# Experts taken in an order by token count, and a shorter router, in a decoder layer on one core

## The chip, the cores and the metric

The kernel runs on one core of a Trainium2 chip. A core has TensorE for matrix products, VectorE, ScalarE and GpSimd (POOL) for element-wise work, and SyncE (SP), which here issues nearly all DMA transfers. The metric is the time of one execution in device microseconds; lower is better.

## The reference, cut to what matters

One layer over 256 tokens of width 1024 in float32: a mixer (gated delta rule and differential attention), a cross-attention over 256 memory tokens, and a mixture of experts, each followed by `x = LN(alpha*x + h)`. The change concerns the end of the second part and the third:

```python
x = layer_norm(DEEPNORM_ALPHA * x + mem_cross_attention(x, mem, ...), ln2_g, ln2_b)
logits = xt @ router_w + router_b                 # 32 experts
top_val, top_idx = lax.top_k(logits, 4)           # 4 experts for each token
gate = softmax(top_val)
h = clamped_swiglu(xb @ w_gate[e] + b_gate[e], xb @ w_up[e] + b_up[e])
y = h @ w_down[e] + b_down[e]                     # for the tokens that chose expert e
x = layer_norm(DEEPNORM_ALPHA * x + sum of gate * y, ln3_g, ln3_b)
```

Each expert has three matrices of 4 MB, 12.6 MB (six halves of 2 MB) in all. With the reference's inputs the 32 experts get 24, 13, 39, 39, 69, 64, 35, 47, 60, 16, 16, 28, 27, 25, 53, 44, 27, 18, 6, 31, 39, 36, 25, 36, 14, 49, 28, 14, 25, 33, 28 and 16 tokens.

## The kernel before, in words

The five engines run five written-out programs, joined by semaphores. Up to the router everything is a fixed list of "units" (`unit_table`): each unit fills one of the eight banks of PSUM from TensorE and is emptied by ScalarE or VectorE; the list's order is TensorE's order and says which bank is free when.

**Cross-attention's end and the router.** The output product W_o has four units of eight products each (`wo0` to `wo3`: two blocks of 128 tokens by two halves of 512 columns). VectorE adds each to the residual (`residual`, L1643) and gathers statistics; `standardise` (L1632) takes the variance, waits for POOL's root (L568) and scales the block. TensorE transposes the scaled block (`x2T0` to `x2T3`), ScalarE and VectorE copy it with gain and bias applied, and eight products for each block give the logits (`route_block`, L1207). Small products on the identity (`keep_warm`, L1217) fill waits. VectorE picks the four largest of 32 (L1705 to L1717). Gains and biases of the block itself are applied by VectorE (block 0, `gains`, L1650) and POOL (block 1, L579 to L581), and TensorE puts alpha times x into four accumulator banks (L1236), where all expert outputs are added later.

**Tables.** A product with a triangle of ones gives each token's position in its expert's list (`pos`, L1241 to L1245). Expert lists are cut into blocks of 32 slots. VectorE counts blocks for each expert (`nblk`, L1741), TensorE sums them up to each expert (`cum`, L1273) and makes a table that says, for each block, whose it is (`etab`, L1287). VectorE writes both tables as integers to `itab` and raises `tab_ready` (L1779). These three small steps are called inside block 0, behind its first, second and fourth eighth of gate and up products (`tables`, L1289), with the transposes of the gates (`GT`) as the second.

**The loop over blocks.** For each block (`work`, L1302) TensorE makes gate and up products (64 of 512 columns, L1318), gathers the next block's tokens (L1255), transposes, adds the previous block's output to the accumulators (L1297), and makes the down products in two passes of 16 (L1359). VectorE and ScalarE do bias, clamp, sigmoid and copies between.

**The loader.** Experts are taken by number, 0 to 31. Weights of even experts go to one set of six slots, of odd experts to another, so two experts are on chip at a time. SP (`load_expert`, L498) reads from `itab` how many blocks come up to and with the expert two before, waits until that many blocks have used the slot, and issues: first halves of gate and up (G0, U0) behind `gu0_used`, second halves (G1, U1) behind `gu_done`, the down halves D0 and D1 behind `d0_used` and `y_done`. The halves of experts 0 and 1 are loaded ahead, at fixed places in cross-attention (L477 to L491), into memory that has come free there. Before the first load of expert 2, SP waits for `tab_ready` (L492).

Of the kernel before, what the change touches and what calls it, by code (L numbers as in the profile page):

```python
# [21 lines left out]
I32 = mybir.dt.int32  # L22
ALU = mybir.AluOpType
# [31 lines left out]
TABLE = 64  # L55
MAX_BLOCKS = N_EXPERTS + SEQ * TOP_K // CAP
# [7 lines left out]
K_ID, K_IOTA, K_UT, K_US, K_ONE, K_CM, K_SOLVE = 0, 128, 192, 320, 448, 576, 960  # L64
N_CONST = K_SOLVE
S_EYE, S_BLOCK, S_LEVT = 0, 256, 260
N_SOLVE = S_LEVT + P * (LEVELS - FIRST_LEVEL)
K_END = K_SOLVE + N_SOLVE


def constants():
# [11 lines left out]
    out[:, K_IOTA:K_IOTA + TABLE] = np.arange(TABLE)  # L83

# [19 lines left out]
def unit_table():  # L104
# [21 lines left out]
    u += [("xs3", "D"), ("vm2", "A"), ("pT0", "A"), ("pT1", "A"), ("vm3", "A"), ("pT2", "A"), ("oT0", "A"), ("oT1", "A")]  # L126
    u += [("pT3", "A"), ("oT2", "A"), ("oT3", "A")]
    u += [("wo0", "D"), ("wo1", "D"), ("wo2", "D"), ("x2T0", "A"), ("x2T1", "A"), ("wo3", "D"), ("bT", "A")]
    u += [("x2T2", "A"), ("x2T3", "D"), ("router", "D")] + [(f"acc{i}", "kept") for i in range(4)]
    u += [("pos", "D"), ("xg0", "A"), ("xgT0", "D"), ("cum", "D"), ("GT", "A"), ("etab", "D")]  # L130
# [6 lines left out]
LAST_USE = {"xgT0": "pos", "cum": "router", "GT": "x2T3", "etab": "GT"}  # L137
# [14 lines left out]
def emptied(name):  # L152
# [12 lines left out]
    ("xa_wo", 0, 1024, 0), ("xa_wo", 0, 1024, 1),  # L165
# [6 lines left out]
ROLE_SLOT = [(N_ATT + r) % SLOTS for r in range(SLOTS)]  # L172
# [6 lines left out]
def trunk_kernel(nc, d, out):  # L179
    ctx = ExitStack()  # L180
    with ctx:
# [32 lines left out]
        small = sb("small", 696)  # L214
        itab = sb("itab", TABLE + 32, I32)

# [41 lines left out]
        iota = kst[:, K_IOTA:K_IOTA + TABLE]  # L258
        levT = {level: ln_mem[:, S_LEVT + P * i:S_LEVT + P * (i + 1)] for i, level in enumerate(range(FIRST_LEVEL, LEVELS))}
# [39 lines left out]
        shift_fin = take(1)  # L299
        top8 = take(16)  # L300
        gsum = take(2)
        nblk, cumc = take(2), take(2)
        rb = take(32)
        eps_rms = take(1)
        minus_half = take(4)
        logit, expl, M, G, pos = (take(64) for _ in range(5))
        assert at[0] <= 696
# [14 lines left out]
        dnw_keep = sb("dnw_keep", 128)  # L322

# [8 lines left out]
        erow = conv_in[0:1, 576:640]  # L332
        mg, mu = (conv_in[:, 256 * i:256 * (i + 1)].rearrange("p (j f s) -> p j f s", j=4, f=2) for i in (4, 5))
        router_w = conv_in[:, 2048:2048 + KC * N_EXPERTS]
        xgT = conv_in[:, 2304:2560].rearrange("p (v h u s) -> p v h u s", v=2, h=2, u=2)
# [10 lines left out]
        T_E, T_CUM = 0, TABLE  # L346
# [30 lines left out]
        ld_cols = sem("ld_cols")  # L377
        gu0_used = sem("gu0_used")
# [24 lines left out]
        rt_in, rt_exp = sem("rt_in"), sem("rt_exp")  # L403
        route_ready = sem("route_ready")
# [27 lines left out]
        def _(sp):  # L432
# [6 lines left out]
            def load_needed_later():  # L439
# [5 lines left out]
                sp.dma_start(ln_mem[:, 0:N_SOLVE], d["consts"][:, K_SOLVE:K_END]).then_inc(ld_lev, 16)  # L445
# [17 lines left out]
            def load_role(role, e, odd, ahead=0):  # L463

                w = d[ROLE_INPUT[role]][0, ahead:].rearrange("e (h p j) n -> e h p (j n)", h=2, j=4)
# [6 lines left out]
            def load_first(role):  # L472
                sp.wait_ge(ring_used, N_ATT + role - SLOTS + 1)
                load_role(role, 0, odd=False)
# [15 lines left out]
            sp.wait_ge(ln_ready, 4)  # L490
# [3 lines left out]
            def blocks_through(e, ahead=0):  # L494

                return sp.value_load(itab[0:1, bass.ds(e + (T_CUM + ahead), 1)], min_val=1, max_val=MAX_BLOCKS)

# [96 lines left out]
        def _(act):  # L594
# [209 lines left out]
            for i in range(3):  # L804
                if i == 2:
                    empty("bT", ebias, as3(2))
# [1083 lines left out]
```

## Time and profile before

| | us |
|---|---|
| median of 3 runs (lowest, highest) | 1252.56 (1250.12, 1252.93) |
| profiled execution, its own time | 1252.49 |
| its span, first to last instruction | 1250.4 |
| TensorE busy | 1089.8 (87%) |
| VectorE busy | 317.5 (25%) |
| ScalarE busy | 189.5 (15%) |
| POOL busy | 35.7 (3%) |
| DMA | 446.56 MB, 357 GB/s over the span |

The page cuts the span into 40 slices of 31.3 us, with the busy share of each engine as a digit (9 is 90% or more). Windows give the same for any stretch, with the granted clock of TensorE as a share of full speed and the DMA's rate. The chain of waits follows the work that ended last back through what released it. A busy share is a mean over stages with different limits.

### The profile page before, as it was taken

Reading aid. Unit: us, or ns where it says so; the run is one execution under the profiler, and the core shown is the slowest. Engines: PE = TensorE matmul, PEld = TensorE weight load, DVE = VectorE, ACT = ScalarE, POOL = GpSimd, SP = SyncE. Lnnn points to the kernel's source line nnn. Section 1 sums busy time; section 2 is a strip of 40 time slices with the busy share of each in tenths; the row PEclk is TensorE's granted clock in tenths of the full one; section 3 lists DMA queues with packets and bytes.
Section 4 is the critical chain, followed back from the end, with each engine's and each line's share of the span. In section 5 each row is a group of like instructions: output and inputs, shape, how many; then the busy total and the mean of one; then the engine's idle time right before and its main releaser. Section 6 shows DMA issues by size and latency. Waiting matters only on the chain.

```text
span 1250.4 us, 19511 instructions
## 1 busy us (share of the span) xinstructions
PE 1089.8 (87%) x7535; PEld 493.7 (39%) x7536; DVE 317.5 (25%) x973; ACT 189.5 (15%) x433; POOL 35.7 (3%) x38
## 2 busy tenths in 40 slices
PE   8999999999899999999966789776699797967885
PEld 6777874965433333333312223222233232322321
DVE  1757433213322222222211122111122221211123
ACT  1231331121111111111100011100011111100111
POOL 0110010100100000000000000000000000000001
PEclk9999999999999999999988799878799898987988
DMA  9733140557899989999999999999999999999995
GB/s 363 275 138 135 68 157 20 202 221 301 347 429 429 429 345 403 408 401 409 428 428 429 429 428 429 430 429 428 428 428 428 428 429 428 429 430 429 428 428 234
DMA packets 43687, 446.56 MB, mean 357 GB/s; under 512 B 6912, under 2 KB 7376, under 8 KB 19088
## 3 DMA queue, kind: packets, MB, share of 16 engines
q1 hardware_dynamic: 39616, 442.43, 84.5%
q10 hardware_dynamic: 4048, 3.81, 1.0%
q8 instruction: 15, 0.25, 0.1%
q14 instruction: 8, 0.07, 0.0%
HBM read 445.18 MB, written 1.05 MB: 357 GB/s over the span
## 4 chain that ended last, share of the span: by engine, by line
PE 60%; DMA 25%; DVE 5%; issue 3%; another core or an unknown queue 2%; DVEq 2%; SPq 1%; POOL 0%; POOLq 0%; ACT 0%; ACTq 0%
DMA main<-in_exp_w_up_dram 24%; PE bank L1318 23%; PE bank L1359 10%; PE bank L882 8%; PE bank L872 6%; PE bank L1255 2%; PE bank L1346 2%; PE bank L1122 2%; DVEq L1807 1%; DVE kst L1813 1%; DVE main L1810 1%; DVE main L1800 1%; PE bank L931 1%; DMA main<-in_w_in_dram 1%
## 5 line engine op out<-in xcount | busy, mean ns | idle before, releaser
L1318 PE MATMUL bank<-main 128*32 128x512 f32 x3008 | 392.0, 676 | 122.2 <-DMA main<-in_exp_w_up_dram 117.7
L1318 PEld LDWEIGHTS bank<-main 128*32 128x32 f32 x3008 | 113.3, 122 | 393.8 <-issue 360.1
L1359 PE MATMUL bank<-main,kst 128*32 128x512 f32 x1504 | 180.8, 598 | 16.9 <-DVE kst L1813 16.9
L1800 DVE TENSOR_TENSOR main<-bank,main 128x256 f32<-128x256 f32 x94 | 39.6, 421 | 590.9 <-PE bank L1346 590.9
L882 PE MATMUL bank<-main 128*128 128x512 f32 x256 | 111.8, 593 | 0.3 <-ACT main L693 0.3
L815 ACT ACTIVATE main<-bank 128x512 f32<-128x512 f32 x47 | 28.1, 598 | 479.2 <-PE bank L1318 479.2
L1297 PE MATMUL bank<-main 64*128 64x512 f32 x384 | 95.4, 615 | 0.7 <-ACT main L823 0.7
L872 PE MATMUL bank<-main 128*128 128x256 f32 x352 | 77.8, 380 | 0.0
L1359 PEld LDWEIGHTS bank<-main,kst 128*32 128x32 f32 x1504 | 39.3, 109 | 90.1 <-issue 64.1
L882 PEld LDWEIGHTS bank<-main 128*128 128x128 f32 x256 | 48.2, 190 | 56.7 <-issue 56.5
L872 PEld LDWEIGHTS bank<-main 128*128 128x128 f32 x352 | 66.5, 190 | 10.1 <-issue 1.1
L1255 PE MATMUL bank<-main,kst 128*32 128x256 f32 x768 | 53.2, 389 | 1.2 <-DVE kst L1733 1.0
L617 ACT ACTIVATE main<-bank 128x512 f32<-128x512 f32 (+2 forms) x51 | 28.2, 578 | 146.5 <-PE bank L872 66.0
L1791 DVE TENSOR_SCALAR main<-kst,small 128x128 f32<-128x128 f32 x94 | 22.7, 284 | 101.4 <-PE bank L1367 99.7
L1297 PEld LDWEIGHTS bank<-main 64*128 64x128 f32 x384 | 33.1, 186 | 29.8 <-issue 22.5
L821 ACT ACTIVATE main<-bank 128x256 f32<-128x256 f32 x47 | 18.0, 383 | 170.7 <-PE bank L1367 170.7
L1255 PEld LDWEIGHTS bank<-main,kst 128*32 128x32 f32 x768 | 27.0, 109 | 38.0 <-issue 28.5
L568 POOL TENSOR_TENSOR small<-small 128x1 f32<-128x1 f32 (+1 forms) x10 | 7.8, 782 | 1088.4 <-DVE small L1833 921.9
L823 ACT ACTIVATE main<-bank 128x512 f32<-128x512 f32 x47 | 28.1, 597 | 70.5 <-PE bank L1359 70.5
L1346 PE MATMUL bank<-kst,main 128*128 128x128 f32 x188 | 35.1, 310 | 0.0
L1346 PEld LDWEIGHTS bank<-kst,main 128*128 128x128 f32 x188 | 26.2, 209 | 20.4 <-issue 20.4
L1261 PEld LDWEIGHTS bank<-kst,main 128*128 128x128 f32 x96 | 15.1, 207 | 36.6 <-issue 35.6
(252 smaller groups left out, 707.0 us busy)
## 6 DMA issues: line engine op xcount, KB each, us to landing
main<-in_exp_w_gate_dram SPq DMA_DIRECT2D x64, 2048.0 KB, 30.2
main<-in_exp_w_up_dram SPq DMA_DIRECT2D x64, 2048.0 KB, 34.7
main<-in_exp_w_down_dram SPq DMA_DIRECT2D x64, 2048.0 KB, 36.7
main<-in_w_in_dram SPq DMA_DIRECT2D x6, 2048.0 KB, 21.8
main<-in_xa_wk_dram SPq DMA_DIRECT2D x2, 2048.0 KB, 10.4
main<-in_w_out_dram SPq DMA_DIRECT2D x2, 2048.0 KB, 10.9
main<-in_xa_wv_dram SPq DMA_DIRECT2D x2, 2048.0 KB, 10.9
main<-in_xa_wq_dram SPq DMA_DIRECT2D x2, 2048.0 KB, 13.7
```

Of the source, the lines that this page charges most:

```text
L617: act.activation(dst, ps[:, :] if src is None else src(ps), func, **kw).then_inc(act_emptied, 1)
L815: act.activation(gu_sb, gu_bank[:, :], ACT.Copy).then_inc(gu_copied, 1)
L823: act.activation(y_sb, y_bank[:, :], ACT.Copy).then_inc(y_copied, 1)
L872: last = pe.matmul(ps[:, j * SEQ:(j + 1) * SEQ], w(k)[:, c * P:(c + 1) * P], src[:, k, :], start=(k == 0), stop=(k == KC - 1))
L882: last = pe.matmul(ps[:, :], srcT[:, k, b * P:(b + 1) * P], w(k)[:, col:col + 512], start=(k == 0), stop=(k == KC - 1))
L1122: last = pe.matmul(ps[:, j * SEQ + b * P:j * SEQ + (b + 1) * P], w(k)[:, (2 * i + j) * P:(2 * i + j + 1) * P], xT[:, k, b * P:(b + 1) * P] ...
L1255: last = pe.matmul(ps[at:at + CAP, 0:256], selw[:, b, :], quarters[:, h, u, :, :], start=(b == 0), stop=(b == 1))
L1297: last = pe.matmul(acc[b][h][:, :], gselT[64 * h:64 * h + 64, b * P:(b + 1) * P], y_sb[64 * h:64 * h + 64, :], start=False, stop=final)
L1318: last = pe.matmul(gu_bank[at:at + CAP, :], xg_chunk(k), weights(role, k, f), start=(k == 0), stop=(k == KC - 1))
L1346: last = pe.transpose(guT_bank[:, j * P:(j + 1) * P], gu_sb.rearrange("p (c j) -> p j c", j=4)[:, j, :], ident)
L1359: last = pe.matmul(y_bank[at:at + CAP, :], hT[:, j, f, :], weights(role, j, h), start=(f == 0 and pair == 0), stop=(f == 1 and pair == 1))
L1800: return tt(dst, gT[:, :, w, :, :], b.unsqueeze(3).broadcast_to([P, 4, 2, CAP]), ALU.add)
```

## The change

- Experts are no longer taken by number. VectorE ranks them by token count (experts 0 and 1 are kept first, ties go to the lower number), a constant row says which rank stands at which position (few and many in turn, the one with fewest last), and the tables get a second row: for each block its position (`T_P`) and its expert (`T_E`), and for SP the expert at each position (`T_ORDER`). Slots go by parity of the position. SP reads one table entry more for each expert.
- The router works on the residual before the norm: its weights are multiplied by LN's gain, their column mean is subtracted (`rw`, a product with ones), the bias part goes into the router's bias, and the logits are scaled by the block's 1/std afterwards. So the transposes don't wait for the norm.
- W_o goes in the order 0, 2, 1, 3 with the transposes between, from two loads cut by columns instead of rows. `keep_warm` is gone, `bT` (biases of the experts) moves ahead to cross-attention.
- Block 0's gains and biases go in two fused instructions on VectorE; block 1 is standardised by ScalarE, and its gains and biases are applied by POOL (lower half) and VectorE (upper half).
- Accumulator sums 1, 2 and 3 move behind `pos` and the gather. The gathered rows are copied by ScalarE. The gates' transposes move behind block 0's gate and up products.
- Early loads: G0 and U0 of expert 0 come behind `xq3`, D0 of expert 1 with its G1 and U1; which memory follows which load is a new list (`ROLE_FOLLOWS`).

```diff
+def rank_at_position():
+    heavy, light = list(range(FIRST_EXPERTS, 16)), list(range(16, N_EXPERTS))
+    last = light.pop()
+    order = list(range(FIRST_EXPERTS))
+    while heavy or light:
+        if light:
+            order.append(light.pop())
+        if heavy:
+            order.append(heavy.pop(0))
+    return np.array(order + [last])
...
+    tie = np.where(e < FIRST_EXPERTS, 1e6 * (FIRST_EXPERTS - e), 0.0) - e
...
-    ("xa_wo", 0, 1024, 0), ("xa_wo", 0, 1024, 1),
+    ("xa_wo", 0, 512, None), ("xa_wo", 512, 512, None),
...
+ROLE_FOLLOWS = [13, 14, 11, 12, 15, 16]
+ROLE_RELEASES = [13, 13, 15, 15, 16, 17]
...
             load_role(G0, 1, odd=True)
+            load_first(G0)
+            load_first(U0)
             sp.wait_ge(unit_filled, UNIT_AT["xs3"] + 1)
             load_role(U0, 1, odd=True)
-            for role in (G0, U0, G1, U1):
-                load_first(role)
+            load_first(G1)
+            load_first(U1)
             sp.wait_ge(unit_filled, UNIT_AT["oT3"] + 1)
             load_role(G1, 1, odd=True)
             load_role(U1, 1, odd=True)
+            load_role(D0, 1, odd=True)
             load_first(D0)
             load_first(D1)
-            sp.wait_ge(unit_filled, UNIT_AT["router"] + 1)
-            load_role(D0, 1, odd=True)
-            sp.wait_ge(ln_ready, 4)
+            sp.wait_ge(ln_ready, 5)
             load_role(D1, 1, odd=True)
             sp.wait_ge(tab_ready, 1)
...
+                done = blocks_through(p, ahead - 2)
+                e = sp.value_load(itab[0:1, bass.ds(p + (T_ORDER + ahead), 1)], min_val=0, max_val=N_EXPERTS - 1)
...
+            root(6, rstd_fin[0])
+            root(7, rstd_fin[1])
+            pool.wait_ge(ld_ln, 64)
+            pool.wait_ge(scaled_x, 1)
+            pool.tensor_tensor(x3[:, 1, 0:HALF], x3[:, 1, 0:HALF], ln_g[:, 0:HALF], ALU.mult)
+            pool.drain()
+            pool.tensor_tensor(x3[:, 1, 0:HALF], x3[:, 1, 0:HALF], ln_b[:, 0:HALF], ALU.add).then_inc(ln_ready, 1)
...
+            arrived(15)
+            ps = begin("wo0")
+            need("oT2")
+            wo_steps(ps, 0, range(0, 6))
+            need("oT3")
+            wo_steps(ps, 0, range(6, 8)).then_inc(unit_filled, 1)
+            wo_steps(begin("wo2"), 2, range(0, 8)).then_inc(unit_filled, 1)
+            need("wo0")
+            tokens_T("x2T", 0, x3)
+            used_up(1, "wo2")
+            arrived(16)
+            wo_steps(begin("wo1"), 1, range(0, 8)).then_inc(unit_filled, 1)
+            need("wo2")
+            tokens_T("x2T", 2, x3)
+            bank_wo3 = begin("wo3")
+            wo_steps(bank_wo3, 3, range(0, 4))
+            need("wo1")
+            tokens_T("x2T", 1, x3)
+            wo_steps(bank_wo3, 3, range(4, 8)).then_inc(unit_filled, 1)
...
+            pe.wait_ge(ln_ready, 5)
             gather(begin("xg0")).then_inc(unit_filled, 1)
+            begin_sum(2)
+            begin_sum(3)
             need("xg0")
             gathered_T(begin("xgT0")).then_inc(unit_filled, 1)
...
                 for k in range(4):
                     last = gate_up(k)
+                    if first and k == 1:
+                        block_counts()
+                last.then_inc(gu0_used, 1)
+                if first:
+                    block_table()
...
+            def choose(b):
+                top = top8[:, 8 * b:8 * b + 8]
+                stt(l3[:, b, :], filled(f"rt{b}")[:, 0:N_EXPERTS], rstd_fin[b], rb, ALU.mult, ALU.add).then_inc(dve_emptied, 1)
+                if b == 1:
+                    stt(offset, mv_fin[1][:, 0:1], -1.0, rstd_fin[1], ALU.mult, ALU.mult).then_inc(offset_in, 1)
...
+            upper_half = slice(HALF, D_MODEL)
+            dve.wait_ge(scaled_x, 2)
+            tt(x3[:, 1, upper_half], x3[:, 1, upper_half], ln_g[:, upper_half], ALU.mult)
+            dve.drain()
+            tt(x3[:, 1, upper_half], x3[:, 1, upper_half], ln_b[:, upper_half], ALU.add).then_inc(ln_ready, 1)
...
+            stt(keys, counts_ps[0:32, 96:128], 64.0, key_row, ALU.mult, ALU.add)
+            stt(own_key, counts_ps[0:32, 64:65], 64.0, key_col, ALU.mult, ALU.add)
+            ts(filling, counts_ps[0:32, 64:65], 1.0 / CAP, None, ALU.mult)
+            dve.drain()
+            dve.sem_inc(dve_emptied, 1)
+            ts(keys, keys, own_key, None, ALU.is_gt)
+            ts(block_steps, iota[0:32, 1:SEQ // CAP], filling, None, ALU.is_lt)
+            dve.drain()
+            dve.reduce_sum(rank, keys, AX_X)
+            dve.reduce_sum(nblk[0:32, 0:1], block_steps, AX_X)
+            dve.drain()
+            stt(at_rank, rank_at[:, 0:32], rank, iota[0:32, 0:32], ALU.is_equal, ALU.mult)
+            ts(at_position, rank_at, rank, None, ALU.is_equal)
```

## Rows read from the trace of the kernel before

**Rows 1.** Page: tenths busy in 40 slices of the span.
```profile
PE   8999999999899999999966789776699797967885
DMA  9733140557899989999999999999999999999995
```
**Rows 2.** Windows: stretch, length; busy PE, PEld, DVE, ACT, POOL; clock, DMA share, GB/s.
```profile
335.00:340.00 5.00, 4.83 (x48) 1.90 (x42) 1.63 (x7) 1.69 (x3) 0.00 (x0) 1.00 0.69 226
340.00:450.00 110.00, 106.47 (x902) 37.94 (x900) 26.79 (x93) 17.51 (x37) 0.00 (x0) 1.00 1.01 428
450.00:620.00 170.00, 165.24 (x1406) 58.76 (x1404) 40.22 (x141) 25.85 (x55) 0.00 (x0) 1.00 0.95 396
620.00:1230.00 610.00, 481.24 (x3586) 160.48 (x3584) 104.47 (x364) 66.58 (x140) 0.00 (x0) 0.89 1.01 429
```
**Rows 3.** Chain of waits: start us, us, what.
```profile
618.70 46.42 DMA main<-in_exp_w_up_dram
1047.08 6.11 PE bank L1318 x32
1223.27 5.06 PE bank L1318 x32
```
**Rows 4.** Chain of waits: down products and gate and up products of full blocks.
```profile
391.56 1.85 PE bank L1359 x16
393.70 7.07 PE bank L1318 x64
422.86 1.85 PE bank L1359 x16
```
**Rows 5.** Timeline of SP: start us, us, line, transfer; first gate halves.
```profile
335.72 0.35 SPq L470 DMA_DIRECT2D main<-in_exp_w_gate_dram  x1
350.90 0.33 SPq L470 DMA_DIRECT2D main<-in_exp_w_gate_dram  x1
413.02 0.33 SPq L470 DMA_DIRECT2D main<-in_exp_w_gate_dram  x1
459.44 0.34 SPq L470 DMA_DIRECT2D main<-in_exp_w_gate_dram  x1
```
**Rows 6.** Timeline from W_o to the tables.
```profile
279.65 20.76 PE L882 MATMUL bank<-main 128*128 128x512 f32 x48
300.25 1.04 PE L864 MATMUL bank<-kst,main 128*128 128x128 f32 x8
308.20 0.69 DVE L1646 SCALAR_TENSOR_TENSOR main<-main,bank 128x512 f32<-128x512 f32 x1 [2.89 <-PE bank L882]
318.19 0.23 DVE L1705 TENSOR_TENSOR small<-bank,small 128x64 f32<-128x64 f32 x1 [1.68 <-PE bank L1211]
320.17 1.96 PE L1236 MATMUL bank<-main,kst 128*128 128x512 f32 x4 [0.22 <-POOL main L581]
321.97 0.30 PE L1241 MATMUL bank<-small,kst 128*128 128x32 f32 x2
323.37 0.51 DVE L1733 TENSOR_SCALAR kst<-kst,small 128x32 f32<-128x32 f32 x2
325.54 0.32 PEld L1261 LDWEIGHTS bank<-kst,main 128*128 128x128 f32 x2 [1.01 <-ACT main L617]
327.27 0.42 DVE L1763 COPY main<-bank 128x256 f32<-128x256 f32 x1
327.80 1.32 PE L1318 MATMUL bank<-main 128*32 128x512 f32 x8 [1.75 <-DVEq L1766]
334.32 0.18 DVE L1777 CAST itab<-main 1x64 int32<-1x64 f32 x1
```
**Rows 7.** Timeline of the end: POOL and VectorE at the same time.
```profile
1243.44 1.25 POOL L590 TENSOR_TENSOR main<-main 128x512 f32<-128x512 f32 x1
1243.64 1.61 DVE L1838 TENSOR_TENSOR main<-main 128x512 f32<-128x512 f32 x1
```
**Rows 8.** DMA issues: transfer, queue, KB, median us to landing.
```profile
main<-in_router_w_dram ACTq DMA_DIRECT2D x1, 128.0 KB, 8.0
```

More of the change, by code:

```diff
@@ L299, in trunk_kernel @@
         shift_fin = take(1)
+        offset = take(1)
         top8 = take(16)
@@ L302, in trunk_kernel @@
         nblk, cumc = take(2), take(2)
+        filling, own_key, rank, position = (take(1)[0:N_EXPERTS, :] for _ in range(4))
         rb = take(32)
@@ L1202, in _ @@
-            last.then_inc(unit_filled, 1)
-            pe.wait_ge(ld_rt, 32)
-            router_ps = begin("router")
-            def route_block(b, parts=()):
-                for k in range(KC):
-                    if k in dict(parts):
-                        need(dict(parts)[k])
-                    last = pe.matmul(router_ps[:, 32 * b:32 * b + 32], xT[:, k, b * P:(b + 1) * P], router_w[:, 32 * k:32 * k + 32],
+            pe.wait_ge(rsum_ready, 1)
+            pe.matmul(begin("rw")[:, 0:2 * N_EXPERTS], ones, router_sums, start=True, stop=True).then_inc(unit_filled, 1)
@@ L1212, in route_block, with wo_steps @@
+            wo_w = [slots[i % SLOTS].rearrange("p k n -> p (k n)").rearrange("p (k n) -> p k n", k=KC) for i in (15, 16)]
+            def wo_steps(ps, i, steps):
+                for k in steps:
+                    last = pe.matmul(ps[:, :], oT[:, k, (i // 2) * P:(i // 2 + 1) * P], wo_w[i % 2][:, k, :],
                                      start=(k == 0), stop=(k == KC - 1))
                 return last
-            warm_bank = begin("acc0")
-            def keep_warm(products):
-                for _ in range(products):
-                    pe.matmul(warm_bank[:, 0:P], ident, ident, start=True, stop=True)
@@ new lines, in _, with route @@
+            need("wo2")
+            tokens_T("x2T", 2, x3)
+            bank_wo3 = begin("wo3")
[3 more added lines that the diff above has]
+            wo_steps(bank_wo3, 3, range(4, 8)).then_inc(unit_filled, 1)
+            def route(ps, b, steps):
+                for k in steps:
+                    last = pe.matmul(ps[:, 0:N_EXPERTS], x2T[b][:, k, :], router_w3[:, k, :], start=(k == 0), stop=(k == KC - 1))
+                return last
@@ new lines, in begin_sum @@
+            def begin_sum(i):
+                pe.matmul(begin(f"acc{i}")[:, :], alpha_eye, x3[:, i // 2, (i % 2) * HALF:(i % 2 + 1) * HALF],
+                          start=True, stop=False).then_inc(unit_filled, 1)
+            need("rw", "x2T1")
+            route(begin("rt0"), 0, range(0, 8)).then_inc(unit_filled, 1)
+            used_up(1, "wo3")
+            need("wo3")
+            tokens_T("x2T", 3, x3)
+            ps = begin("rt1")
+            need("x2T2")
+            route(ps, 1, range(0, 4))
@@ L1248, in gather @@
+            pe.matmul(ps[0:32, 96:128], ones[:, 0:32], M[:, 32:64], start=False, stop=True).then_inc(unit_filled, 1)
+            begin_sum(1)
             def gather(ps):
```

331 lines of the change are left out of this document (187 added, 144 removed).

## The prediction

> **What bounds the kernel now.** I read the 40 slices of the page first. TensorE looks like the bound (nines almost throughout), but from slice 21 on its digits fall to 6 or 7 in between while DMA stays at 9 [rows 1]. The share of 87% is an average over two regimes. The table of windows separates them: in 620 to 1230 us the DMA moves 429 GB/s without a gap and TensorE works 481 of 610 us; in 450 to 620 us TensorE works 165 of 170 us and the DMA falls to 396 GB/s [rows 2]. So the expert stage is first bound by TensorE and then by the weights.
>
> Two durations follow. One expert of weights (six transfers of 2 MB): in the chain of waits TensorE resumes on the landing of an expert's second up half at 1047.08 and at 1223.27 [rows 3]; by the reference's routing these are six experts apart, so 176.2 / 6 = 29.37 us per expert, 4.9 us per transfer. One block of 32 token slots, where nothing is waited for: the second pass of down products starts at 391.56 and the next but one at 422.86 [rows 4], so 15.65 us. There are 47 blocks: 47 x 15.65 = 736 us of TensorE against 32 x 29.37 = 940 us of DMA. On the whole the stage is the DMA's, and every idle microsecond of the DMA in it is lost.
>
> Where is it idle? SP's queue shows it. The first gate half of an expert is issued at 350.90, 413.02 (two further) and 459.44 [rows 5]: 62.1 and 46.4 us apart, which is 2 + 2 and 3 blocks, since the slot is released by the last block of the expert two before. I worked the counts out from the reference: experts 0 to 31 need 1,1,2,2,3,2,2,2,2,1,1,1,1,1,2,2,1,1,1,1,2,2,1,2,1,2,1,1,1,2,1,1 blocks. Experts 2 to 8 hold 15 blocks in a row, 235 us of TensorE against 206 us of weights. Only two experts fit on chip, so the loader runs against full slots and the DMA stops. Later single-block experts let TensorE wait (46.42 us at 618.70 [rows 3]), but the DMA's lost time doesn't come back.
>
> How much: from the first load after the tables, issued at 335.72 [rows 5], to the landing at 1223.27 lie 887.55 us. In it stand 30 experts less the two down halves of the last, 30 x 29.37 - 9.8 = 871.3. The rest, 16.2 us, is the latency of the first transfer and idleness. In 335 to 340 us the DMA moved 226 GB/s x 5 us, 2.6 us of stream at 429 [rows 2], so it began at 337.4 and the latency is 1.6: 14.6 us idle. The other way, (429 - 396) / 429 x 170 = 13.1 us in 450 to 620. I take 14.
>
> **The change, part by part.** *Order.* With experts 0 and 1 kept first, the sort gives by blocks 1,1 then 1,3,1,2,1,2,... and at the end 1,1 (14 of the experts left have two blocks or more, 16 one). A pair costs the DMA 58.7 us and TensorE 3 x 15.65 = 47.0, the first pair 62.6. Does the DMA meet a full slot? Let a heavy expert land at T. Its first block ends about T + 2; a last block of two starts then and frees the first gate/up half a quarter of a block later (7.07 / 2 us [rows 4]), T + 6; of three, T + 21. The loader needs that slot when the light expert behind it has been moved, at T + 29.4: slack 23 and 8 us. The second gate/up half is freed 3.5 us after the first and needed 9.8 us after it, the last down half is freed 12 and needed 24.5 us after it: more slack, not less. So no idleness is left from the third expert on, and the 14 us go. What is late next is the DMA itself, at 29.37 us per expert. If the 8 us of slack behind the one expert of three blocks were gone, it would cost what lies over it, once.
>
> *End.* The last three positions have 2, 1, 1 blocks, as experts 29, 30, 31 have now. The last up half lands, then 27.1 us to the end of the span (1250.4 - 1223.27). It stays; I allow 1.5 us for the clock, since the 32 products behind the landing took 5.06 and 6.11 us in two such places [rows 3] and half of 7.07 where nothing was waited for [rows 4].
>
> *Head.* The loads of experts 2 and on can't begin before the tables are on chip; so what counts is when SP issues its first load, now 335.72. The steps:
> 1. The eight bias transposes go ahead of W_o and a small product joins them: TensorE reaches W_o, now at 279.65, 1.0 + 0.2 us later (eight transposes took 1.04 at 300.25 [rows 6]); W_o keeps its 27.7 us (20.76 for three of four), and three sets of four transposes instead of two stand between its parts (0.5 more). The last residual starts near 309.9 instead of 308.20.
> 2. From there to the logits it now takes 10.0 us (308.20 to 318.19 [rows 6]): statistics, root on POOL, standardising, transposes, four gained copies, 16 products. After: addition 0.7, transposes 0.5, two halves of a plain copy 0.4 each, the last products 0.3 and a switch between engines behind each: about 3.5; VectorE's own way there (statistics and the first block's choice, 0.7 + 0.6 + 1.5 behind the addition) is as long. Logits of the second block at 313.6, 4.6 us earlier.
> 3. From the logits to the counting product at 321.97 it is 3.8 us, of them 1.96 behind a pair of accumulator sums that waited for POOL's gains (till 320.17), so choosing is 1.8; after, it is 1.6 for the second block alone: 315.2. The counting product follows at once.
> 4. But VectorE now does a half of the second block's gains before it copies the positions: two of 0.69 us (as at 308.20 [rows 6]), behind ScalarE's two passes over x (0.6 each, from 314.0). POOL does the other half meanwhile. At 1243.64 such an instruction took 1.61 us with POOL's 1.25 beside it [rows 7]. So 317.1 to 318.9, then copy and selection (0.9): 318.0 to 319.8 against 323.88 [rows 6].
> 5. Between gather and its transposes stand two accumulator sums, 1.96 us [rows 6] where 0.5 was idle: 1.4 later. The copy of the gathered rows goes from VectorE, where it waited behind the gates until 327.27 though the transposes of 325.54 took 0.5, to an idle ScalarE: 1.2 earlier. Block 0 starts at 322.5 to 324.3 instead of 327.80, 3.5 to 5.3 earlier; I take 3.8, near the contended end, as step 4's row is of that case.
> 6. In block 0 the gates' transposes leave the way to the tables (two, by the eight at 300.25 some 0.3, and two switches); three tiny products, a table row of twice the width and a second table read on SP's way (now 1.2 us from 334.50 [rows 6] to 335.72 [rows 5] with one read) join it: I count these as even, each side is about 1 us. The new rank arithmetic on VectorE, some 13 instructions of 0.13 to 0.2 us with as many drains, is 2.5 to 3 us and lies beside the gather, the transposes and the first two eighths of block 0; if this cover were gone it would delay the tables by itself.
> Sum: the first load 3.8 us earlier, at 331.9. Bounds: steps 4 and 6 at their best give 6.3. At worst nothing is won; and below it, the router weights (issued at 260.20 on ScalarE's queue, now with two more expert loads beside them) must be there, scaled and summed before W_o at 281; the nearest row, an 8.0 us landing [rows 8], leaves some 10 us, so I put -1 as the lower end. The expert loads moved ahead (two at about 255, a down half at 281) fill time in which the DMA idles (digits 5 to 7 in the eighth to tenth slice [rows 1]) and are landed long before block 1; nothing is worth anything there, as SP then waits for the tables. Gains and biases later in block 0 (gates after the tables) delay that block's tail, not the loader, which has 19.6 us of halves queued by then.
>
> **Sum.** 14 + 3.8 = 17.8; span 1250.4 - 17.8 = 1232.6. The profiled execution took 1252.49, 2.09 over its span, and the median is 1252.56, the same. Predicted time 1234.7 us, a ratio of 0.986.
>
> **Rivals.**
> *A, the order brings little.* If experts don't come out in turns (ties, a wrong key), or the stop moves to the slots behind the three-block expert, most of the 14 us stays and only the head is won: 1248.7; with half of it, 1241.7. For it: two experts of slack is short, and the three-block one comes at the very start, when no lead has built up. Against: 8 us of slack by the above. 8%.
> *B, no change.* The idleness stays and the first load isn't earlier because the longer table chain eats it: 1252.5. 4%.
> *C, slower: the clock.* In turns, TensorE waits for weights before every expert, where it now runs 280 us at full clock (1.00 in 340 to 620, 0.89 after [rows 2]). Behind each wait products run at half speed for a while: 32 of them took 5.06 to 6.11 instead of 3.5 us [rows 3, 4]. It decides from the point where a pair's three blocks exceed 58.7 us, a mean block of 19.6 instead of 15.65. At full half speed, 1.2 instead of 2.4 GHz, three blocks would be 94 us, and 15 pairs 530 us over the DMA. Against it: a TensorE that doesn't wait has the full clock (1.00 in 340 to 450), so the loss limits itself; the surplus seen is 1.5 to 2.6 us per 32 products, at most some 6 per expert, 47 + 12 = 59 at the very worst. At that limit some pairs lose a few us: with 20 us lost, 1255.6. 5%.
> The Trainium skill, "TensorE: Matmul & The Clock Gate", section "HAM oscillation — how this bites in real kernels", says that a DMA wait in every turn of a loop makes each turn start cold, and counts it as lost time; by that rule alone the order would cost. The trace agrees on the cold starts, but here they lie in time that the DMA sets anyway.
>
> **Chances.** Forecast 83%, A 8%, B 4%, C 5%. Range for 8 in 10: head 6.3, idleness 14.6 and an end 1.5 shorter give 1230.1; head -1, idleness 11 and 1.5 the other way give 1244. All bounds at once are rare on either side, and half of A lies at 1241.7: 1230.5 to 1241.5. Within 0.2% (2.5 us, what a measurement can tell here: the three runs spread over 2.8) is B and a part of A: 5%. Slower 5%, faster 90%.
>
> **What would show it.** Right: DMA windows at 429 GB/s from about 340 to the end, none at 396; SP's first load after the tables near 332; TensorE waiting some 12 us per pair all through the stage, with a mean clock below 1.00 already in 350 to 620; the last up half landing near 1205.5; 27 us after it. Wrong: a window of the DMA below 420 behind the three-block expert; landings of the last experts more than 29.4 us apart; a first load later than 335.7; or gate/up products at half clock in heavy experts' second blocks.

## The result and the profile after

The changed kernel takes 1239.45 us (median of 4, 1238.71 to 1240.66), the kernel before 1251.61 us beside it (median of 4): a ratio of 0.9903 [0.9891, 0.9916]. It is faster by 1.0%; the forecast was 1234.7 us, inside the range of 1230.5 to 1241.5, and 4.7 us too fast: a gain of 17.8 us was forecast and 12.2 came. A second measurement of the same file, taken later, gave 1238.67 us and 0.9889 [0.9872, 0.9905]; its trace is called the control below.

The page of the changed kernel, the two rows that stand in [rows 1] for the kernel before:
```profile
PE   7999999999898999788887979797969797888874
DMA  9643121578599999999999999999999999999995
```
TensorE's digits leave the nines at slice 17 and alternate from slice 22 on, where before it had nines to slice 20 and sixes and sevens among the digits behind: the waiting is spread over the stage. The DMA's nines begin in slice 12, as before.

Windows of the changed kernel (columns as in [rows 2]):
```profile
335.00:350.00 15.00, 12.18 (x87) 4.45 (x82) 5.03 (x19) 4.05 (x7) 0.00 (x0) 0.89 0.97 388
350.00:450.00 100.00, 93.22 (x784) 33.20 (x780) 22.40 (x78) 14.28 (x30) 0.00 (x0) 0.98 1.01 428
450.00:620.00 170.00, 144.87 (x1168) 50.64 (x1160) 33.62 (x117) 21.42 (x45) 0.00 (x0) 0.95 1.01 429
620.00:1000.00 380.00, 321.39 (x2498) 110.99 (x2502) 73.46 (x254) 46.61 (x98) 0.00 (x0) 0.92 1.01 428
1000.00:1190.00 190.00, 162.33 (x1276) 55.94 (x1270) 35.68 (x127) 23.39 (x50) 0.00 (x0) 0.92 1.01 428
```
Between 450 and 620 us stood 396 GB/s with TensorE busy for 165 of 170 us [rows 2]; now 429 GB/s and 145 us. Behind 350 us no window of the stage has a hole. TensorE's clock is below 1.00 in all of them, from 0.98 down to 0.92, and the DMA's rate doesn't suffer by it.

Chain of waits of the changed kernel, at its first and last experts (start, length, what):
```profile
356.59 31.02 DMA main<-in_exp_w_up_dram
387.75 5.06 PE bank L1404 x32
401.26 7.06 PE bank L1404 x64
...
1172.72 37.10 DMA main<-in_exp_w_up_dram
1209.96 5.25 PE bank L1404 x32
```
The last up half lands at 1209.96, where it was 1223.27 [rows 3]; then 27.3 us to the end, as before 27.1.

The whole difference fits in three terms, each read from SP's first load behind the tables, the last landing and the span:

```
                      first load   last landing   span    stage    tail
before                  335.72       1223.27     1250.4   887.55   27.1
changed                 334.79       1209.96     1237.3   875.17   27.3
changed, control        333.72       1208.71     1236.8   874.99   28.1
```
With the control: 2.0 us of head, 12.6 us of stage, and 1.0 us given back in the tail, 13.6 in all. The stage repeats to 0.2 us, the tail only to 0.8. The head of the first trace was 1.1 us worse: already W_o began at 283.05 in it and at 281.11 in the control, against 279.65 before [rows 6], so some 2 us of lateness at W_o belong to that execution and not to the change.

### The profile page after: what moved, and what is told of

Its sections match the earlier page's. It is cut to its first block, busy times and chain, and to the rows that moved or that the text cites. A ratio compares the mean times of both kernels' runs of the same rounds, so it can differ in the third digit from the quotient of the medians.

```text
span 1237.3 us, 19683 instructions
## 1 busy us (share of the span) xinstructions
PE 1085.1 (88%) x7525; PEld 494.6 (40%) x7526; DVE 321.3 (26%) x982; ACT 189.4 (15%) x429; POOL 33.6 (3%) x38
## 4 chain that ended last, share of the span: by engine, by line
PE 50%; DMA 42%; DVE 3%; DVEq 1%; issue 1%; ACTq 1%; SPq 1%; ACT 1%; POOL 0%; PEldq 0%
DMA main<-in_exp_w_up_dram 41%; PE bank L1404 17%; PE bank L933 6%; PE bank L1448 6%; PE bank L943 6%; PE bank L1264 2%; PE bank L1183 2%; PE bank L1335 2%; PE bank L992 1%; PE bank L1435 1%; PE bank L973 1%; ACTq L847 1%; DVEq L1941 1%; DVE kst L1947 1%; DVE main L1944 1%
## 5 line engine op out<-in xcount | busy, mean ns | idle before, releaser
L1404 PE MATMUL bank<-main 128*32 128x512 f32 x3008 | 385.4, 666 | 112.6 <-DMA main<-in_exp_w_up_dram 110.8
L876 ACT ACTIVATE main<-bank 128x512 f32<-128x512 f32 x47 | 28.1, 598 | 459.5 <-PE bank L1404 459.1
L943 PE MATMUL bank<-main 128*128 128x512 f32 x192 | 84.0, 593 | 0.3 <-ACT main L746 0.3
L933 PEld LDWEIGHTS bank<-main 128*128 128x128 f32 x352 | 66.4, 190 | 10.2 <-issue 1.1
L943 PEld LDWEIGHTS bank<-main 128*128 128x128 f32 x192 | 36.0, 190 | 42.4 <-issue 42.3
L884 ACT ACTIVATE main<-bank 128x512 f32<-128x512 f32 x47 | 28.1, 597 | 70.5 <-PE bank L1448 70.5
## 6 DMA issues: line engine op xcount, KB each, us to landing
main<-in_xa_wk_dram SPq DMA_DIRECT2D x2, 2048.0 KB, 10.3
```

The costliest lines, as they stand in the source:

```text
L876: act.activation(gu_sb, gu_bank[:, :], ACT.Copy).then_inc(gu_copied, 1)
L884: act.activation(y_sb, y_bank[:, :], ACT.Copy).then_inc(y_copied, 1)
L933: last = pe.matmul(ps[:, j * SEQ:(j + 1) * SEQ], w(k)[:, c * P:(c + 1) * P], src[:, k, :], start=(k == 0), stop=(k == KC - 1))
L943: last = pe.matmul(ps[:, :], srcT[:, k, b * P:(b + 1) * P], w(k)[:, col:col + 512], start=(k == 0), stop=(k == KC - 1))
L1404: last = pe.matmul(gu_bank[at:at + CAP, :], xg_chunk(k), weights(role, k, f), start=(k == 0), stop=(k == KC - 1))
```

## The experiments

**The order alone.** The changed kernel with all of its new head, and the experts by number:
```diff
-    return np.array(order + [last])
+    return np.arange(N_EXPERTS)
...
-            stt(keys, counts_ps[0:32, 96:128], 64.0, key_row, ALU.mult, ALU.add)
+            stt(keys, counts_ps[0:32, 96:128], 0.0, key_row, ALU.mult, ALU.add)
```
(the expert's own key likewise).

> The changed kernel with experts at positions by number, as before; router, head and table chain stay as changed. Theory O (the order keeps the DMA busy, the head gave 1 to 3 us): the 12.4 us that passed less between first load and last landing come back, 1250 to 1252 us, and the DMA falls below 429 GB/s in 450 to 620 us again. Rival H (the gain is the shorter head, the order does nothing): 1239.5 us, like the changed kernel.

1252.3 us, 1.0005 [0.9996, 1.0015]. Windows and chain of waits of this kernel:
```profile
450.00:620.00 170.00, 165.34 (x1408) 60.27 (x1406) 40.48 (x142) 25.76 (x54) 0.00 (x0) 1.00 0.95 394
```
```profile
1222.22 6.51 PE bank L1404 x32
```
The hole of the kernel before is back, 394 GB/s against 396 [rows 2], and the stage is 887.92 us (first load 334.30). So the order is worth 12.9 us (874.99 against 887.92), the whole of the gain, and the loader's stop goes and comes with it. The head's 1.4 us are in the trace, but the tail is 28.6 us instead of 27.1: the 32 products behind the last landing took 6.51 us where they took 5.06 [rows 3]. The head as built, with the tail as it fell out here, is worth nothing that could be measured in the total.

**The order turned round.** Same key, but positions in descending count, all experts with many tokens first:
```diff
-    return np.array(order + [last])
+    return np.arange(N_EXPERTS)
```

> The changed kernel with the ranks taken straight: experts 0 and 1, then by falling token count. Theory O: 14 experts with 29 blocks stand together, 31.3 us of TensorE each against 29.37 us of weights, so the loader meets full slots; the load of position 17 begins near 795 instead of 777 us, 18 us of idleness: 1256 to 1258 us, worse than by number. Rival H: 1239.5. Rival S (any sorting by count helps, as it balances the stages): below 1245.

1264.62 us, 1.0108 [1.0091, 1.0124], slower than before, and 7 to 9 us above what I expected; that any sorting by count would do is refuted. Windows:
```profile
350.00:450.00 100.00, 97.65 (x830) 35.93 (x822) 24.14 (x83) 15.67 (x33) 0.00 (x0) 1.00 0.96 404
450.00:620.00 170.00, 165.39 (x1408) 60.50 (x1406) 40.33 (x142) 26.15 (x55) 0.00 (x0) 1.00 0.97 403
620.00:800.00 180.00, 174.97 (x1484) 63.27 (x1484) 43.71 (x153) 27.15 (x58) 0.00 (x0) 1.00 0.98 409
```
TensorE is nearly full and at clock 1.00, and the DMA short all the way to 800 us. Against 429 GB/s the three windows lack 5.8, 10.3 and 8.4 us, 24.5 in all, and the stage is 25.0 us longer than the control's (899.94 against 874.99). The work and the bytes are those of the changed kernel; only who stands behind whom differs. I had computed 18 us of idleness; the 7 that are missing no run took apart.

**More work in each block.** To find how far the turns carry, the gather is done three times instead of once in every block behind the first, with the same result; first in the changed kernel, then in the kernel before:
```diff
                 pe.wait_ge(gselT_ready, n + 1)
+                for _ in range(2):
+                    gather(xg_bank)
                 gather(xg_bank).then_inc(xg_done, 1)
```

> The changed kernel with the gather of every block made three times (32 more products of 256 columns, 2.2 us of TensorE for each block, 104 us in all; the result is the same). Theory O: a pair's three blocks are 53.7 us, still under the 58.7 us of two experts' weights, so only the last block's 2.2 us, behind the last landing, show: 1241.7 us (up to 1243). Rival C (TensorE with its half clock behind each wait is close to the bound): 1250 or more.

> The kernel before with the same 2.2 us of work more for each block. Theory O: in the stretch of experts 2 to 8 with the blocks around it TensorE is the bound, some 16 blocks, 35 us more of idle DMA, and 2.2 us at the end: 1284 to 1290 us. Rival (the DMA sets the time in this kernel too, its pauses don't matter): 1254 us.

1248.01 us, 0.9971 [0.996, 0.9983], in the changed kernel, where I expected 1241.7; 1290.79 us, 1.0315 [1.0297, 1.0332], in the one before. A block of the changed kernel took 17.4 us in it (gate and up products at 372.63, 390.02, 407.45, 425.03). That is 1.75 us more in each of 46 blocks, 80 us of TensorE at full clock; it costs the kernel before 39 us and the changed one 8.5 to 10.3 (0.9971 against 0.9903 and 0.9889). Windows of the changed kernel with more work:
```profile
415.00:420.00 5.00, 5.00 (x53) 2.59 (x45) 1.44 (x5) 1.17 (x3) 0.00 (x0) 1.00 1.01 429
420.00:425.00 5.00, 4.64 (x38) 1.37 (x37) 2.29 (x9) 0.39 (x1) 0.00 (x0) 1.00 0.81 344
425.00:430.00 5.00, 5.00 (x52) 3.11 (x52) 0.00 (x0) 0.60 (x1) 0.00 (x0) 1.00 0.03 10
430.00:435.00 5.00, 5.00 (x70) 3.16 (x62) 0.00 (x0) 0.60 (x1) 0.00 (x0) 1.00 0.97 360
```
One hole, 6.7 us by these rows, at one place: behind the only expert of three blocks, whose slot is free at 429.00. The rest of the stage is whole (429 GB/s in 450 to 620 us). The stage is 6.3 us longer than the control's and the tail 2.2 us, which is the whole cost; the expectation had only the tail. Window of the kernel before with more work:
```profile
450.00:620.00 170.00, 165.79 (x1572) 63.62 (x1568) 37.30 (x130) 23.78 (x50) 0.00 (x0) 1.00 0.78 325
```
At 325 GB/s this window lacks 41 us, where it lacked 13 without the work [rows 2]: 28 of the 39 us stand in it alone.

**Over the pair.** The same with six gathers in a block, to pass the point at which the turns should stop helping:

> The changed kernel with the gather of each block made six times (5.5 us of TensorE more for each block, 21.2 us; same result). Theory O with its point at a mean block of 19.6 us: a pair's 63.6 us now exceed the DMA's 58.7, TensorE is the bound from the third position to the thirtieth, 42 blocks x 21.2 us from about 375, then two more blocks: 1318 to 1330 us, with the clock at 1.00. Rival C (the clock's loss comes on top in each pair): over 1350.

1299.81 us, 1.0372 [1.0355, 1.039]. Chain of waits and windows:
```profile
480.88 7.07 PE bank L1404 x64
487.96 5.53 PE bank L1335 x89
...
501.03 7.05 PE bank L1404 x64
...
1264.63 7.07 PE bank L1404 x64
```
```profile
620.00:1000.00 380.00, 371.64 (x3946) 158.64 (x3941) 70.84 (x247) 44.90 (x95) 0.00 (x0) 1.00 0.99 416
1000.00:1230.00 230.00, 225.10 (x2370) 94.68 (x2366) 42.30 (x149) 27.14 (x57) 0.00 (x0) 1.00 0.99 418
```
A block is 20.1 us and not the 21.2 I had assumed (six gathers in a row take 5.5 us, 0.92 each, not 1.11), so a pair is 60.4 us against the DMA's 58.7, and now TensorE is the bound: 98% busy, clock 1.00, the DMA at 416 to 418 GB/s. That takes 46 us off the expectation, which is more than it missed by: it also counted a block too few, 44 from 375 us on where the trace has 45, which begin from 380.24 to 1264.63. With 45 blocks of 20.1 us its sum gives 1290 to 1302. The crossing lies between 17.4 and 20.1 us per block, and the 19.6 of the prediction is in between; no run puts it closer. And the clock, 0.92 where the DMA sets the pace, is 1.00 as soon as TensorE does: the slower clock didn't bring the bound nearer.

**Three parts of the head.** Each changes one thing between the last residual and the first load. First, twelve products of the identity with itself into a free bank, six before the wait for the second block's choice and six behind the second accumulator sum, in place of those that the change took out:
```diff
+            def keep_warm(products):
+                ps = begin("acc2")
+                for _ in range(products):
+                    pe.matmul(ps[:, 0:P], ident, ident, start=True, stop=True)
+
+            keep_warm(6)
             pe.wait_ge(alpha_ready, 1)
...
             begin_sum(1)
+            keep_warm(6)
```

> The changed kernel with twice six small products on the identity, after the logits of the second block and after the second accumulator sum (the changed kernel has none; the one before had twelve). Theory K (the clock fell to half at 315.8 us in the changed kernel's trace and stayed there to 325.6; gather and sums 2 and 3 took 1.93 and 2.63 us instead of 1.11 and 1.96, and these lie on the way to the first load): the clock is 1.00 by the gather, the first load comes 1.5 us earlier, 1238.0 us. Rival (VectorE and the lock with POOL set this stretch alone): the first load doesn't move, 1239.5. Rival (the products themselves delay the position product): up to 1.5 us later, 1241.

Second, the last accumulator sum behind the transposes of the gathered rows instead of ahead of them (the list of units and banks likewise):
```diff
             begin_sum(2)
-            begin_sum(3)
             need("xg0")
             gathered_T(begin("xgT0")).then_inc(unit_filled, 1)
+            begin_sum(3)
```

> The changed kernel with accumulator sum 3 behind the transposes of the gathered rows instead of ahead of them, where it fills the wait for ScalarE's copy. Theory: one sum of 1.3 us at half clock leaves the way to block 0: the first load 1.0 to 1.3 us earlier, 1238.3. Rival (sum 3 then stands in the way of block 0 itself): no change, 1239.5.

Third, SP waits for the table that it reads (offsets and order), not for the table of blocks that comes three VectorE instructions and a visit to TensorE later:
```diff
-            sp.wait_ge(tab_ready, 1)
+            sp.wait_ge(cum_ready, 1)
...
             dve.sem_inc(dve_emptied, 1)
+            dve.sem_inc(cum_ready, 1)
```

> The changed kernel where SP waits for the table that it reads (blocks up to each position, expert at each position, written by 330.44 us) and not for the table by blocks (written by 332.92). SP's first load then waits for gate and up's first half of block 0 (about 332.1). Theory D (the stage is the DMA's from its first load on, and each microsecond that this load comes earlier is a microsecond of the whole): first load 2.0 to 2.5 us earlier, 1237.2 us. Rival R (the DMA only starts sooner and stops again behind the expert of three blocks, whose slot in the changed kernel was free 4 us before it was needed): first load as said, but less than 1 us of the whole.

And the three together:

> The three last edits together. Theory D: block 0 2.5 to 2.8 us earlier by the warm clock and the late sum, 2.0 to 2.5 by the early table, 4.5 to 5.3 in all: 1234.5 us. Rival R: the stop behind the expert of three blocks takes part of it back (its slack was 4 us; block 0's end doesn't come earlier by as much): 1236 to 1237 with a DMA window below 420 GB/s between 410 and 425 us.

On one chip, on which the unchanged head was not run: 1236.7 us, 0.9885 [0.987, 0.9901]; 1239.17 us, 0.9891 [0.9876, 0.9906]; 1235.98 us, 0.9868 [0.9853, 0.9883]; together 1234.14 us, 0.9851 [0.9838, 0.9865]. The late sum shows nothing. The early table brings the first load 4.6 us behind block 0's start (327.73 to 332.32) instead of 7.0 (326.71 to 333.72 in the control), 2.4 us, and its median lies 3.2 us under the late sum's. Its stage is 875.2 us, so the slot behind the expert of three blocks wasn't met. With the identity products three of four times lie at 1236.3 to 1236.7, the fourth at 1240.5, and the interval overlaps that of the control (0.9889 [0.9872, 0.9905]); so the trace has to carry that verdict: the first load is at 331.28, 2.4 us before the control's. Windows of the control and then of the kernel with identity products:
```profile
308.00:318.00 10.00, 9.23 (x60) 6.54 (x58) 7.43 (x22) 2.43 (x5) 2.89 (x3) 1.00 0.57 210
318.00:320.00 2.00, 0.00 (x0) 0.00 (x0) 1.85 (x5) 0.00 (x0) 0.24 (x1) 0.78 0.00 0
320.00:326.00 6.00, 5.67 (x22) 2.22 (x22) 2.16 (x16) 0.38 (x1) 0.00 (x0) 0.50 0.90 339
```
```profile
318.00:326.00 8.00, 6.92 (x52) 3.40 (x50) 4.26 (x19) 0.77 (x2) 0.49 (x1) 1.00 0.66 240
```
In the control TensorE stands still for some 3 us before the gather, and its clock goes from 1.00 to 0.50, which is 1.2 GHz; with the identity products it stays at 1.00. Standing still isn't all there is to it: in the first trace of the changed kernel the clock fell already at about 315.8 us, and over 315 to 319 us, with TensorE busy for 4.00 of 4 us, it was 0.57. Nor is the clock certain to stay up with the products: in the profiled execution of the three together it fell before they began, and stayed down through the first six. Windows of that execution:
```profile
315.00:326.00 11.00, 11.00 (x54) 8.59 (x57) 7.44 (x28) 1.77 (x3) 2.59 (x2) 0.55 0.65 244
```
That execution was the slowest of its five, 1238.13 us where the others took 1232.62 to 1234.38.

**POOL's part.** The control and, on the same chip, the changed head with the second block's lower half of the gains on VectorE as well:
```diff
-            pool.wait_ge(scaled_x, 1)
-            pool.tensor_tensor(x3[:, 1, 0:HALF], x3[:, 1, 0:HALF], ln_g[:, 0:HALF], ALU.mult)
-            pool.drain()
-            pool.tensor_tensor(x3[:, 1, 0:HALF], x3[:, 1, 0:HALF], ln_b[:, 0:HALF], ALU.add).then_inc(ln_ready, 1)
...
+            dve.wait_ge(scaled_x, 1)
+            tt(x3[:, 1, lower_half], x3[:, 1, lower_half], ln_g[:, lower_half], ALU.mult)
+            dve.drain()
+            tt(x3[:, 1, lower_half], x3[:, 1, lower_half], ln_b[:, lower_half], ALU.add).then_inc(ln_ready, 1)
```

> The changed kernel unchanged, as a control beside the three others. All theories: 1239.5 us. Its trace tells whether the 2 us by which everything stood later in its first trace (xa_wo issued at 227.81 instead of 225.84) belong to the change (it comes back) or to that execution (it is gone, as in four of the other traces), and whether the half clock from 315.8 to 325.6 us comes back.

> The changed kernel with all four gain and bias instructions of the second block on VectorE, none on POOL. In the changed kernel's trace VectorE's two small subtractions took 1.40 us and the first half product 1.79 with POOL's two instructions beside them. Theory L (the shared port holds VectorE back for as long as POOL's help saves): both back at 0.37 and 0.69, two more of 0.69 and two drains, the selection 0.3 us earlier to 0.3 later, time 1239.5 as before. Rival (POOL's help is real): 1.5 us slower, 1241.

1238.67 us for the control, 1236.44 us, 0.9876 [0.986, 0.9893], without POOL's help. The control's four times (1238.38 to 1238.79) and this kernel's four (1236.04 to 1238.14) don't overlap. VectorE does two instructions more and is done earlier. Timeline of the control, POOL and VectorE from the second block's choice to the selection:
```profile
315.48 1.40 DVE L1837 TENSOR_SCALAR small<-small 128x32 f32<-128x32 f32 x2
315.52 1.32 POOL L632 TENSOR_TENSOR main<-main 128x512 f32<-128x512 f32 x1 [2.65 <-ACT main L867]
316.98 1.26 POOL L634 TENSOR_TENSOR main<-main 128x512 f32<-128x512 f32 x1
317.00 1.79 DVE L1842 TENSOR_TENSOR main<-main 128x512 f32<-128x512 f32 x1
318.86 0.69 DVE L1844 TENSOR_TENSOR main<-main 128x512 f32<-128x512 f32 x1
319.77 0.51 DVE L1855 TENSOR_SCALAR kst<-kst,small 128x32 f32<-128x32 f32 x2
```
and of the kernel without POOL's part:
```profile
315.38 0.38 DVE L1832 TENSOR_SCALAR small<-small 128x32 f32<-128x32 f32 x2
315.88 0.69 DVE L1838 TENSOR_TENSOR main<-main 128x512 f32<-128x512 f32 x1
318.92 0.51 DVE L1855 TENSOR_SCALAR kst<-kst,small 128x32 f32<-128x32 f32 x2
```
Two small subtractions take 1.40 us with POOL's multiplication beside them and 0.38 alone, a product 1.79 and 0.69: VectorE loses 2.1 us to be spared a multiplication and an addition of 0.69 each. The first load is at 331.64, 2.1 us earlier: the selection 0.85, and 1.2 more because the two accumulator sums behind the gather took 2.60 us where the control's took 3.78, with the clock back sooner (0.79 over 318 to 326 us against 0.57).

**The best of these.** Identity products and the early table, on that same chip:

> The changed kernel with the identity products and the early table, without the late sum (which showed nothing). Theory D: the two gains add up where they lie one behind the other: the first load waits for block 0's first half, which the warm clock brings 1.5 to 2 us earlier; against the control 4 to 5 us less, 1234.5 to 1235.5. Rival (block 0's first half is late either way): no better than the early table alone.

1233.7 us (1232.96 to 1234.54), 0.985 [0.9834, 0.9867], 5.0 us under the control and 1.5% under the kernel before. Timeline of its gather and block 0, and of SP:
```profile
321.12 1.11 PE L1343 MATMUL bank<-main,kst 128*32 128x256 f32 x16 [0.61 <-DVE kst L1863]
324.84 1.92 PE L1412 MATMUL bank<-main 128*32 128x512 f32 x16 [0.47 <-ACT main L671]
...
329.46 0.34 SPq L515 DMA_DIRECT2D main<-in_exp_w_gate_dram  x1
```
The first load is 4.3 us earlier than the control's, the stage takes 874.97 us as there, the tail 27.3 where the control's was 28.1. So 0.8 of the 5.1 us of span between the two traces is the tail's, which none of the edits touches. On this chip the first load was at 333.72, 331.64 and 329.46 in three kernels and the span 1236.8, 1234.3 and 1231.7; the stage was 875.0 to 875.7 us in all eight traces of this order without the added gathers, so a microsecond of the first load is one of the last landing. The version without POOL's part was not joined to this one; whether the two add up stays open.

## Why the prediction was nearly right, by its steps

The forecast span was 1232.6 us and the control's is 1236.8: 1.4 us of the difference are in the order, 1.8 in the head, 1.0 in the tail.

**What bounds the stage.** Right. Undoing the order alone gives the time of before back (1.0005), and the holes go and come with it. Two figures were off. The 46.42 us at 618.70 are a transfer from issue to landing and not a wait of TensorE, whose three waits for landings in that stretch are 5.48, 5.84 and 4.18 us. And TensorE waits 8.7 us per pair in 450 to 620 us and not 12, since it works part of the time at the lower clock.

**The order, 14 us.** The mechanism held, the size was 12.6 (12.9 against the order by number). I had two readings: 14.6 from the stage less the moved bytes and 1.6 of latency, and 13.1 from the window of 396 GB/s. The second was nearly exact. The first counts as idleness what no window shows as a hole: the changed kernel's stage still holds 874.99 - 871.3 - 1.6 = 2.1 us over that sum, and 1 GB/s, the rounding of a window's rate, is 2 us in 875. I should have taken the window's.

**The slack behind the three-block expert, 8 us.** Wrong by half, without consequence. The stream of 388 GB/s in 335 to 350 us is 13.6 us at 429, so it began at 336.4. Three experts later, at 424.5, it wanted the slot. SP issued that gate half at 420.55, 4.0 us ahead. The failed step is "its first block ends about T + 2". By the stream T is 336.4 + 58.7 = 395.1, and the second block's products start at 401.26, T + 6. Two things make up the difference: the up half with which the stream was done at 385.3 counts as landed at 387.61, 2.3 us later, and the 32 products behind it took 5.06 us at the lower clock and not 3.5. With blocks of 17.4 us this slack was overdrawn by the 6.7 us of idleness; 4 us more of it would have cut that to 2.7.

**The end.** Even in the first trace (27.3), 1.0 longer in the control (28.1) and 1.5 by number (28.6): at most the 1.5 that I allowed. It hangs on the clock behind the last landing, 5.06 to 6.51 us for the same 32 products.

**The head, 3.8 us.** 2.0 in the control, 0.9 in the first trace. By its steps, against the control:
1. W_o at 281.11, 1.5 later and not 1.2; the last residual at 310.25, forecast 309.9. Right.
2. Logits at 314.21, forecast 313.6, against 318.19 [rows 6]. Right: the router on the residual does shorten this way, by 4.0 us of the 4.6 forecast.
3. and 4. The contended end of my range for the end of the selection was 319.8; it began at 319.77 and ended at 320.28, 0.5 later, and 0.6 had come with the logits. That it lay so near is in part luck: I had charged the sharing to one instruction, and it stopped VectorE twice, the first time in two subtractions of 32 columns, 1.40 us for 0.38. [rows 7] had shown this only for two wide tensors. The Trainium skill, "SBUF — State Buffer", section "SBUF: two separate sides", says that VectorE and GpSimd share one pair of ports, that one instruction holds the pair to its end while the other engine is blocked, and that on VectorE's side instructions with two inputs in SBUF and those in a two-port performance mode take it. The trace agrees in that the subtractions end at 316.88 and POOL's multiplication at 316.84, and the 1.79 us run 0.55 past the end of POOL's addition; whether the subtractions, which have one tensor as input, ran in such a mode no run here shows.
5. The failed step. Block 0 started at 326.71 and not by 324.3. I had written gather, sums and transposes with the durations of before, at full clock (1.11 and 1.96 us, [rows 6] for the latter). Timeline of the control:
```profile
320.33 1.94 PE L1335 MATMUL bank<-main,kst 128*32 128x256 f32 x16 [2.88 <-DVE kst L1855]
322.19 3.78 PE L1295 MATMUL bank<-main,kst 128*128 128x512 f32 x4
```
At 0.50 the gather took 1.94 us and the sums 3.6 to the start of the next product, 2.5 us more in all; with the 0.5 of step 4 that is more than the 2.4 by which block 0 was late, because the step's own terms add up to 322.1 to 323.9 where I wrote 322.5 to 324.3. The kernel before had products of no use in the gaps to its choice, and its clock was 1.00 from 315 to 328 us; the diff takes them out, and I listed them neither as a cost nor as a cover. In the kernel with identity products the gather takes 1.11 us again, the sums 1.98, and block 0 starts at 324.31.
6. Tables: from block 0's start to the first load 7.0 us instead of 7.9. That is 0.9 better than even, but by the clock and not by the chain. Window and timeline of the kernel before, then of the control:
```profile
328.00:332.00 4.00, 4.00 (x26) 0.85 (x22) 0.49 (x3) 0.04 (x1) 0.00 (x0) 0.57 0.91 389
329.37 1.94 PE L1318 MATMUL bank<-main 128*32 128x512 f32 x8
```
```profile
328.00:332.00 4.00, 4.00 (x46) 1.25 (x42) 1.05 (x6) 0.00 (x0) 0.00 (x0) 1.00 0.00 0
328.98 1.92 PE L1404 MATMUL bank<-main 128*32 128x512 f32 x16
```
Before, eight products took as long as sixteen in the control: some 1.0 us lost in the slow stretch of block 0, and 0.2 in the gates' transposes behind it (0.69 us, 0.44 at 334.71 in the control). At an equal clock the new chain is then about 0.3 us longer. From the end of the table's last copy to the first load it is 1.9 us, 1.2 before; SP's second read stands in between, and no run prices it by itself.
Sum of the control: block 0 1.1 us earlier, tables 0.9, 2.0 together. The forecast had 3.8 and 0. So without the slow stretch of before the head would have come out at about 0.8.

**Rivals.** A (the order brings little) and B (no change) are refuted by the experts by number against the changed kernel. C (slower through the clock) was priced from a point that the runs allow: the stage turns to TensorE's bound between 17.4 and 20.1 us per block, where I had put 19.6 (its own time should have read 1254.7, 1234.7 and 20, and not 1255.6). Its cause is refuted: the mean clock of 0.92 belongs to the waiting, and when the waiting goes it is 1.00. The rule that I set beside it, from the Trainium skill, "TensorE: Matmul & The Clock Gate", section "HAM oscillation — how this bites in real kernels", holds here as a description and not as a price in this stage. In the first trace 26 of 27 starts behind a landing took 4.95 to 6.48 us for 32 products; the one behind a wait of 1.28 us took 3.64. Where it did cost is the head, in step 5, where TensorE is on the path and the DMA isn't.

## What to carry to other kernels

In a loop that loads ahead into few slots, compare compute and transfer over as many steps as there are slots, not over the whole loop, and put costly steps between cheap ones; here that is 13 us of 1250 with the same work and bytes. When an edit takes out filler work on TensorE, price every product up to the next long stretch at both clock levels. Where a loader's start sets everything behind it, let it wait for the one table that it reads, and see whether another engine's work beside it slows down the engine that it waits for.

## What the runs showed of the hardware

- POOL's multiplication of 512 columns held up VectorE's subtractions of 32 columns, which have one tensor as input: 1.40 us for two, 0.38 alone. Giving the work to one engine was faster than halving it.
- The clock over the same identity products was 1.00 in two kernels. In a third it was 0.50 from 315 to 324 us, though TensorE was busy all the time, and back at 1.00 in 325. What brought it down before them, at about 315 us, no run shows.
- Gathers in a row took 0.92 us each at clock 1.00, one by itself 1.11.
- Two executions of one file differed by 1.9 us at W_o. Half of it was there at the very start: the first products with w_in, which wait for its load, began at 9.06 us in the first trace and at 8.12 in the control (8.04 in the kernel before). Where 2 us are in question, one trace of each kernel is too little; most of the head's readings above rest on one trace each.
